# Moving the modulation's columns behind the memory's last products in a two-block transformer kernel

## The chip, the cores and the metric

One core of one Trainium2 chip runs the whole program. The metric is device time in microseconds (us) of one execution.

## What is computed

The program is two blocks in a row, for one sequence of 256 tokens of width 2048, in 32-bit floats. Everything below concerns the start of it. Cut to what matters there:

```
mem_n = rms_norm(mem, mem_norm_w)                       # 256 x 2048
k0, v0, k1, v1 = mem_n @ mem_k0, mem_n @ mem_v0, ...    # four 2048 x 512 matrices ("the memory's products")
mod = silu(c) @ w_ada + b_ada                           # 2048 x 6144, c is one vector
shift, scale, gate = split(mod, 3)
h = rms_norm(x, norm_gain) * (1 + scale) + shift
proj = h @ w_in                                         # 2048 x 8192 ("layer 1's products")
... attention, retention, w_out, x + gate * y, then the second block's two layers, which use k0..v1
```

The memory's products need nothing of the modulation, so they run first and cover the loading and adding up of w_ada. Layer 1's products need `h`, and with it shift and scale.

## The kernel before

**Products.** Every product on TensorE (PE) goes by chunks of a weight matrix of 512 KB: one DMA on SP's queue brings it into one of 7 slots of `raw` (`load_weights`, L393), ScalarE (ACT) rounds it into `w_hi` (`split_hi`, L414, instruction L418; 5 slots), VectorE (DVE) writes the rest into `w_lo` over the raw slot (`split_lo`, L420, instruction L422), and PE multiplies by both (L486 to L488 where the products have tokens as rows, L492 and L493 elsewhere). ACT and DVE split chunk n+3 while chunk n is multiplied (`AHEAD = 3`). SP asks for chunk n when PE is through chunk n-7.

**Units.** A chunk of PE's is here called a unit. The memory's products (`G_MEM`) are units 0 to 31, of 2 MB for each of the four matrices; layer 1's products begin with unit 32 (`G_SBQK0`), and their first 40 units use the first half of the rows of `h` only. In every unit, ACT, DVE and PE run a hook beside the chunk's work: `mem_hook_1` (L771) on ACT, `ada_hook` (L1299) on DVE, `mem_tail_hook` (L1890) on PE. Each engine runs its instructions in the order in which they were written.

**The modulation.** w_ada comes as 96 transfers of 512 KB ("modulation chunks") on POOL's queue (L615), into a ring of 6 tiles, each asked for when the sixth before it is used (semaphore `ada_used`). DVE adds each, weighted by silu(c), into `ada_sum` (L1257 for a first, L1260 for the others). The first 32 chunks are shift and scale of the first 8 tiles of `h` (half 0), the next 32 those of the other 8 tiles, the last 32 are the gate. `ada_units` (L1289) says how many are added by which unit. After a half's last chunk PE turns the sums into columns by 32 matmuls with one column (`modulation_columns`, L1881, instruction L1876), and `half_norm` on DVE and ACT makes 8 tiles of `h`: DVE reads the columns (L1278, L1279), computes a tile (L1157), ACT rounds it (L689), DVE writes the rest (L1166). A tile's L1166 comes two tiles later than its L1157, and the first product of layer 1 waits for tiles 0 to 3.

**The norm of x.** x comes as 4 transfers (L614) on POOL's queue, ahead of modulation chunks 10, 12, 14 and 16; ACT squares them in four groups (L659), POOL adds up three of them (L596, L598) between its transfers, PE sums over partitions (L1862), and ACT makes the inverse root (L677, L680).

In the memory's products the order of all this is a matter of unit numbers:

```
done.append(done[-1] + (3 <= u < units - 3) + (4 <= u < units - 4 and u % 4 == 0))   # ada_units, L1289
if u == MEM_UNITS - 4:                                                               # mem_tail_hook
    modulation_columns(0)
if u >= units - 3:                                                                   # ada_hook, and the like on ACT
    half_norm(half, u - (units - 3))
```

So before, one chunk is added in each of the units 3 to 28, and a second one in the units 4, 8, 12, 16, 20 and 24; PE's columns stand behind unit 28, and `half_norm(0)` is spread over the units 29 to 31.

Of the kernel before, what the change touches and what calls it, by code (L numbers as in the profile page):

```python
# [148 lines left out]
def build(nc, io):  # L149
    with ExitStack() as ctx:  # L150
# [411 lines left out]
        def _(sp):  # L562
# [14 lines left out]
            for g in ORDER:  # L577
                load_weights(sp, g, beside_first if g is G_MEM[0] else None)
                if g is G_SBQK:
                    sp.wait_ge(q["ada_cols"], 2)  # L580
                    sp.dma_start(con1[:, :], io["con1"]).then_inc(loaded["con1"], 16)
# [8 lines left out]
        def _(pool):  # L590
# [11 lines left out]
            for m, (half, k, part) in enumerate(ADA_ORDER):  # L602
# [5 lines left out]
                if m in (22, 25, 28):  # L608
                    add_squares(1, [(22, 25, 28).index(m)])
# [32 lines left out]
        def _(act):  # L642
# [128 lines left out]
            def mem_hook_1(unit):  # L771
                if unit in (0, 2, 4):
                    mem_hi(unit // 2 + 1)
                if unit in (0, 1, 3, 5):
                    norm_square(0, (0, 1, 3, 5).index(unit), mem_raw)
                if unit == 7:
                    mem_root()
                if unit in (17, 19, 21, 23):
                    act.wait_ge(loaded["x"], 64)
                    norm_square(1, (17, 19, 21, 23).index(unit), xT)  # L780
                if unit == 26:
                    norm_inverse_root(1)
                if unit >= MEM_UNITS - 3:
                    half_norm(0, unit - (MEM_UNITS - 3))
# [15 lines left out]
            for i, g in enumerate(G_MEM):  # L800
                run(g, at_units(8 * i, mem_hook_1), hook_first=False)
            for i, g in enumerate((G_SBQK0, G_RTQK0, G_SBV0)):
                run(g, at_units(16 * i, early_hook), hook_first=False)
# [343 lines left out]
        def _(dve):  # L1147
# [141 lines left out]
            def ada_units(units):  # L1289

                done = [0]
                for u in range(units):
                    if units == MEM_UNITS:
                        done.append(done[-1] + (3 <= u < units - 3) + (4 <= u < units - 4 and u % 4 == 0))
# [4 lines left out]
            def ada_hook(u0, units, half):  # L1299
                done = ada_units(units)  # L1300

                def hook(b, p):
                    if p % 2 == 0:
# [5 lines left out]
                        if u >= units - 3:  # L1309
                            half_norm(half, u - (units - 3))  # L1310
                return hook

            for i, g in enumerate(G_MEM):
                run(g, ada_hook(8 * i, MEM_UNITS, 0), hook_first=False)
            for i, g in enumerate((G_SBQK0, G_RTQK0, G_SBV0)):
# [529 lines left out]
        def _(pe):  # L1845
# [44 lines left out]
            def mem_tail_hook(i, p):  # L1890
# [13 lines left out]
                if u in (19, 21, 23, 25):  # L1904
                    sum_squares(1, [(19, 21, 23, 25).index(u)])
                if u == MEM_UNITS - 4:
# [386 lines left out]
```

## Time and profile before

| | us |
|---|---|
| time, median of 3 runs | 1797.61 (1795.02 to 1800.67) |
| time of the profiled execution | 1793.41 |
| its span, first to last instruction | 1791.2 |
| TensorE busy in the span | 1742.6 (97%) |
| VectorE busy | 1288.3 (72%) |
| ScalarE busy | 899.7 (50%) |
| GpSimd busy | 125.9 (7%) |
| mean granted TensorE clock | 0.991 of full |
| moved by DMA | 350.70 MB |

The busy shares are averages over the whole program. All of the change lies in its first 130 us, where they are different ones, so the rows below are nearly all of that stretch. Times in rows count from the start of the span; PE is TensorE, DVE VectorE, ACT ScalarE, POOL GpSimd, SP the engine that only issues transfers. A timeline's row may merge neighbours that overlap: "x2" is two instructions, and its second number is the time that they take together.

### The profile page before, as it was taken

How to read it: one execution, taken by the hardware profiler on the slowest of the kernel's cores; microseconds unless marked ns; L12 is line 12 of the kernel's file. 1: busy time of each engine (PE TensorE's matmuls, PEld its weight loads, DVE VectorE, ACT ScalarE, POOL GpSimd, SP SyncE). 2: the span in 40 equal slices, each digit the busy share in tenths (PEclk: the TensorE clock that was granted, in tenths of full speed). 3: DMA queues.
4: the chain of work that ended last, by engine and by line, in shares of the span. 5: the costliest groups of instructions: out<-in, count | busy, mean ns of one | idle time of the engine just before them, and what ended most of it. 6: DMA issues, size and time to landing. Idle time of an engine off the chain costs nothing.

```text
span 1791.2 us, 24344 instructions
## 1 busy us (share of the span) xinstructions
PE 1742.6 (97%) x9671; PEld 1496.0 (84%) x9671; DVE 1288.3 (72%) x1622; ACT 899.7 (50%) x1161; POOL 125.9 (7%) x151
## 2 busy tenths in 40 slices
PE   7989999999999999999999999899999999999997
PEld 6778888877888888888888888788888888888885
DVE  6889979785677756887676777965554766778644
ACT  6444443444466445665444556654444545566532
POOL 3321101000010100110000000000000000000000
PEclk9989999999999999999999999999999999999998
DMA  9979979774445566666544555555565564444552
GB/s 359 385 270 349 343 233 326 230 237 136 146 147 175 188 177 188 189 186 178 165 142 141 155 162 166 167 188 188 188 184 176 161 204 141 141 130 131 176 187 96
DMA packets 310400, 350.70 MB, mean 196 GB/s; under 512 B 11296, under 2 KB 284832, under 8 KB 310288
## 3 DMA queue, kind: packets, MB, share of 16 engines
q1 hardware_dynamic: 295728, 296.24, 53.8%
q0 software_dynamic: 14560, 52.89, 8.2%
q8 instruction: 78, 1.28, 0.3%
q14 instruction: 34, 0.28, 0.1%
HBM read 347.00 MB, written 2.10 MB: 195 GB/s over the span
## 4 chain that ended last, share of the span: by engine, by line
PE 67%; DVE 18%; ACT 6%; issue 5%; DMA 2%; SPq 0%; ACTq 0%; DVEq 0%
PE psG L492 37%; PE psG L493 19%; DVE w_lo L422 6%; ACT w_hi L418 3%; DMA raw<-in_mem_w 2%; PE psG L486 2%; PE psG L488 2%; PE psG L487 2%; DVE ada_sum L1260 1%; DVE P L1218 1%; DVE P L1213 1%; PE psH L1876 1%; DMA ada_ring<-in_w_ada 1%; PE psH L1862 1%; DVE gate_sum L1260 1%
## 5 line engine op out<-in xcount | busy, mean ns | idle before, releaser
L492 PE MATMUL psG<-xA,w_hi 128*128 128x512 f32 x2624 | 942.2, 402 | 4.2 <-DVE w_lo L422 3.7
L422 DVE TENSOR_TENSOR w_lo<-raw,w_hi 128x1024 fp32r<-128x1024 f32 (+1 forms) x560 | 688.5, 1240 | 245.5 <-ACT w_hi L418 244.0
L493 PE MATMUL psG<-xA,w_lo 128*128 128x256 f32 x2624 | 734.5, 280 | 0.0
L418 ACT ACTIVATE w_hi<-raw 128x1024 fp32r<-128x1024 f32 (+1 forms) x560 | 570.4, 1043 | 234.9 <-PE psG L493 167.3
L492 PEld LDWEIGHTS psG<-xA,w_hi 128*128 128x128 f32 x2624 | 492.4, 188 | 123.1 <-issue 10.5
L493 PEld LDWEIGHTS psG<-xA,w_lo 128*128 128x128 f32 x2624 | 495.5, 189 | 4.2 <-issue 3.4
L492 PE MATMUL psG<-yP,w_hi 128*128 128x512 f32 x960 | 337.2, 396 | 3.1 <-DVE P L1218 1.6
L493 PE MATMUL psG<-yP,w_lo 128*128 128x256 f32 x960 | 267.9, 279 | 0.0
L492 PEld LDWEIGHTS psG<-yP,w_hi 128*128 128x128 f32 x960 | 180.0, 187 | 45.9 <-DVE P L1218 1.9
L461 ACT ACTIVATE P<-psG 128x512 f32<-128x512 f32 (+2 forms) x103 | 60.9, 592 | 241.3 <-PE psG L493 241.0
L493 PEld LDWEIGHTS psG<-yP,w_lo 128*128 128x128 f32 x960 | 181.0, 189 | 0.2
L1213 DVE TENSOR_TENSOR P<-psG,P 128x512 f32<-128x512 f32 (+2 forms) x103 | 70.4, 684 | 114.7 <-ACT P L461 114.7
L1260 DVE SCALAR_TENSOR_TENSOR ada_sum<-ada_ring,silc,ada_sum 128x1024 f32<-128x1024 f32 x60 | 79.9, 1338 | 0.0
L596 POOL TENSOR_TENSOR W<-W 128x512 f32<-128x512 f32 x15 | 28.1, 1871 | 645.2 <-ACT W L659 645.2
L615 POOL DMA_DIRECT2D ada_ring<-in_w_ada x96 | 51.1, 533 | 305.8 <-DVE gate_sum L1260 124.0
L1233 DVE TENSOR_TENSOR xT<-psG,xT 128x512 f32<-128x512 f32 x32 | 22.1, 692 | 54.3 <-PE psG L493 53.8
L492 PE MATMUL psG<-xM,w_hi 128*128 128x512 f32 x128 | 49.4, 425 | 3.3 <-DVE w_lo L422 3.3
L486 PE MATMUL psG<-w_hi,xA 128*128 128x512 f32 x128 | 52.0, 406 | 0.0
L492 PE MATMUL psG<-xQ,w_hi 128*128 128x512 f32 x144 | 51.1, 399 | 0.0
L487 PE MATMUL psG<-w_lo,xA 128*128 128x512 f32 x128 | 50.6, 395 | 0.0
L488 PE MATMUL psG<-w_hi,xA 128*128 128x512 f32 x128 | 50.5, 395 | 0.0
L693 ACT ACTIVATE xA<-xT,vec 128x256 fp32r<-128x256 f32 x32 | 14.3, 501 | 52.0 <-DVE xT L1236 27.3
(325 smaller groups left out, 1789.9 us busy)
## 6 DMA issues: line engine op xcount, KB each, us to landing
raw<-in_w_in SPq DMA_DIRECT2D x360, 512.0 KB, 3.8
raw<-in_w_out SPq DMA_DIRECT2D x128, 512.0 KB, 3.4
ada_ring<-in_w_ada POOLq DMA_DIRECT2D x96, 512.0 KB, 6.3
raw<-in_mem_w SPq DMA_DIRECT2D x32, 512.0 KB, 10.1
raw<-in_w_uq SPq DMA_DIRECT2D x24, 384.0 KB, 3.3
raw<-in_w_ukv SPq DMA_DIRECT2D x32, 128.0 KB, 2.4
raw<-in_w_ukv SPq DMA_DIRECT2D x16, 256.0 KB, 3.3
P<-in_memT SPq DMA_DIRECT2D x4, 512.0 KB, 7.1
```

The costliest lines, as they stand in the source:

```text
L418: nc.scalar.activation(high(n), low(n, raw), ACT.Copy).then_inc(hi_ready, 1)
L422: nc.vector.tensor_tensor(low(n), low(n, raw), high(n), ALU.subtract).then_inc(lo_ready, 1)
L461: nc.scalar.activation(g.dst(b), product(g, b, 0), ACT.Copy).then_inc(copied, 1)
L486: nc.tensor.matmul(out, x_hi, hi[:, w], start=first, stop=False)
L487: nc.tensor.matmul(out, x_hi, lo[:, w], start=False, stop=False)
L488: last = nc.tensor.matmul(out, x_lo, hi[:, w], start=False, stop=end)
L492: nc.tensor.matmul(psG[:, bank + f, :], hi[:, w], x, start=first, stop=False)
L493: last = nc.tensor.matmul(psG[:, bank + f, S:2 * S], lo[:, w], x[:, 0:S], start=False, stop=end)
L596: nc.gpsimd.tensor_tensor(a[:, 0:512], a[:, 0:512], a[:, 512:1024], ALU.add).then_inc(q["nm_pair"], 1)
L615: pool.dma_start(ada_ring[slot][:, :], ada_rows(k, part, half)).then_inc(ada_loaded[slot], 16)
L1213: ins = v.tensor_tensor(out, product(g, b, 1), out, ALU.add)
L1260: v.scalar_tensor_tensor(out=out, in0=src, scalar=silc[:, k:k + 1], in1=out, op0=ALU.mult, op1=ALU.add).then_inc(ada_used, 1)
```

## The change

- `ada_units`: half 0's chunks are added one in each of the units 3 to 31, and a second one in the units 14, 19 and 24.
- PE's `modulation_columns(0)` stands behind unit 31 instead of unit 28.
- All three steps of `half_norm(0)`, on ACT and DVE, stand behind unit 31 instead of in the units 29, 30 and 31.
- The squares of x are taken by ACT in the units 17, 19, 22, 24 (before 17, 19, 21, 23), the third group added by POOL ahead of modulation chunk 27 (before 28), summed by PE in the units 21, 23, 25, 27 (before 19, 21, 23, 25), and the root taken in unit 28 (before 26).
- SP waits, ahead of its first transfer for layer 1 (chunk 32), until 24 modulation chunks have been used.

No instruction is added or taken away but SP's wait.

```diff
             load_memory(0)
             for g in ORDER:
+                if g is G_SBQK0:
+                    sp.wait_ge(ada_used, 24)
                 load_weights(sp, g, beside_first if g is G_MEM[0] else None)
...
-                if m in (22, 25, 28):
-                    add_squares(1, [(22, 25, 28).index(m)])
+                if m in (22, 25, 27):
+                    add_squares(1, [(22, 25, 27).index(m)])
...
-                if unit in (17, 19, 21, 23):
+                if unit in (17, 19, 22, 24):
                     act.wait_ge(loaded["x"], 64)
-                    norm_square(1, (17, 19, 21, 23).index(unit), xT)
-                if unit == 26:
+                    norm_square(1, (17, 19, 22, 24).index(unit), xT)
+                if unit == 28:
                     norm_inverse_root(1)
-                if unit >= MEM_UNITS - 3:
-                    half_norm(0, unit - (MEM_UNITS - 3))
...
             for i, g in enumerate(G_MEM):
                 run(g, at_units(8 * i, mem_hook_1), hook_first=False)
+            for step in range(3):
+                half_norm(0, step)
...
                     if units == MEM_UNITS:
-                        done.append(done[-1] + (3 <= u < units - 3) + (4 <= u < units - 4 and u % 4 == 0))
+                        done.append(done[-1] + (3 <= u) + (u in (14, 19, 24)))
...
-                        if u >= units - 3:
+                        if half and u >= units - 3:
                             half_norm(half, u - (units - 3))
...
             for i, g in enumerate(G_MEM):
                 run(g, ada_hook(8 * i, MEM_UNITS, 0), hook_first=False)
+            for step in range(3):
+                half_norm(0, step)
...
-                if u in (19, 21, 23, 25):
-                    sum_squares(1, [(19, 21, 23, 25).index(u)])
-                if u == MEM_UNITS - 4:
+                if u in (21, 23, 25, 27):
+                    sum_squares(1, [(21, 23, 25, 27).index(u)])
+                if u == MEM_UNITS - 1:
                     modulation_columns(0)
```

DVE's order around half 0's last chunks. Before (`ada_ring_67` is the ring's tile of chunk 31, the last of half 0; L422 are splits, L1278 and L1279 read the columns):

```order
L422 TENSOR_TENSOR w_lo<-raw,w_hi 128x1024 [waits hi_ready]
L1260 SCALAR_TENSOR_TENSOR ada_sum<-ada_ring_67,silc,ada_sum 128x1024 [waits ada_used,ada_loaded1]
L422 TENSOR_TENSOR w_lo<-raw,w_hi 128x1024 [waits hi_ready]
L1278 TENSOR_TENSOR mod<-psH,vec 128x2x8 [waits ada_cols]
L1279 SCALAR_TENSOR_TENSOR gs<-mod,vec 128x8 [waits dve_step]
L1157 SCALAR_TENSOR_TENSOR W<-xT,gs,W 128x256 [waits nm_rs,dve_step]
L1157 SCALAR_TENSOR_TENSOR W<-xT,gs,W 128x256 x2
```

And in the changed kernel, whose lines from L577 on have moved by two or more:

```order
L1262 SCALAR_TENSOR_TENSOR ada_sum<-ada_ring_71,silc,ada_sum 128x1024 [waits ada_used,ada_loaded5]
L422 TENSOR_TENSOR w_lo<-raw,w_hi 128x1024 [waits hi_ready]
L1262 SCALAR_TENSOR_TENSOR ada_sum<-ada_ring_66,silc,ada_sum 128x1024 [waits ada_used,ada_loaded0]
L422 TENSOR_TENSOR w_lo<-raw,w_hi 128x1024 [waits hi_ready]
L1262 SCALAR_TENSOR_TENSOR ada_sum<-ada_ring_67,silc,ada_sum 128x1024 [waits ada_used,ada_loaded1]
L1215 TENSOR_TENSOR memkv<-psG,memkv 128x512 [waits copied]
L1220 TENSOR_TENSOR memkv<-memkv,P 128x512 [waits nm_rs,dve_step]
L1280 TENSOR_TENSOR mod<-psH,vec 128x2x8 [waits ada_cols]
L1281 SCALAR_TENSOR_TENSOR gs<-mod,vec 128x8 [waits dve_step]
```

Before, the last addition stands behind the split of chunk 31. Now it stands behind the split of chunk 34, a chunk of layer 1's weights, and the landing of the memory's last block (L1215, L1220) stands between it and the columns.

PE's order around the columns, before (`xM` is the normed memory, so the products behind are unit 29's):

```order
L492 MATMUL psG<-xM,w_hi 128x512
L493 MATMUL psG<-xM,w_lo 128x256
L1876 MATMUL psH<-con,ada_sum 128x1 [waits ada_used]
L1876 MATMUL psH<-con,ada_sum 128x1 x15
L492 MATMUL psG<-xM,w_hi 128x512 [waits lo_ready,nm_lo]
```

And in the changed kernel (`xA` is `h`, so the products behind are unit 32's):

```order
L492 MATMUL psG<-xM,w_hi 128x512
L493 MATMUL psG<-xM,w_lo 128x256
L1880 MATMUL psH<-con,ada_sum 128x1 [waits ada_used]
L1880 MATMUL psH<-con,ada_sum 128x1 x15
L492 MATMUL psG<-xA,w_hi 128x512 [waits lo_ready,nm_lo,vector_landed]
```

The products behind the columns are now the ones that wait, by `nm_lo`, for the tiles of `h` that are made from the columns.

## Rows read from the trace of the kernel before

**Rows 1.** Windows: stretch and length, then busy us of PE, PEld, DVE, ACT, POOL; clock; DMA share; GB/s.

```profile
60.00:110.00 50.00, 44.29 (x203) 36.92 (x204) 48.59 (x39) 24.84 (x28) 21.02 (x26) 0.93 1.04 380
118.00:126.00 8.00, 8.00 (x36) 7.21 (x37) 5.32 (x13) 3.22 (x7) 0.00 (x0) 0.66 0.03 10
130.00:240.00 110.00, 110.00 (x617) 95.68 (x616) 97.02 (x98) 50.90 (x61) 15.32 (x29) 0.98 0.93 322
```

**Rows 2.** Waits, 40 to 125 us: who waited for whom, total us, times, longest.

```profile
ACT w_hi L418 <- DMA raw<-in_mem_w: 27.6, 11, 5.0
PE psG L492 <- DVE w_lo L422: 3.3, 1, 3.3
PE psH L1862 <- POOL W L598: 2.8, 1, 2.8
PE psH L1876 <- DVE ada_sum L1260: 2.5, 1, 2.5
```

**Rows 3.** PE's timeline: start, length, instruction, [idle before it and releaser].

```profile
59.16 0.28 PE L493 MATMUL psG<-xM,w_lo 128*128 128x256 f32 x1
62.75 0.76 PE L492 MATMUL psG<-xM,w_hi 128*128 128x512 f32 x1 [3.32 <-DVE w_lo L422]
...
102.09 0.58 PE L492 MATMUL psG<-xM,w_hi 128*128 128x512 f32 x1
...
110.48 0.28 PE L493 MATMUL psG<-xM,w_lo 128*128 128x256 f32 x1
113.25 6.98 PE L1876 MATMUL psH<-con,ada_sum 128*128 128x1 f32 x32 [2.49 <-DVE ada_sum L1260]
120.10 0.77 PE L492 MATMUL psG<-xM,w_hi 128*128 128x512 f32 x1
...
130.05 0.40 PE L492 MATMUL psG<-xA,w_hi 128*128 128x512 f32 x1
```

**Rows 4.** Windows again, columns as in rows 1: two stretches at a lower clock.

```profile
62.00:69.00 7.00, 6.25 (x19) 5.32 (x20) 7.00 (x7) 3.40 (x5) 1.58 (x3) 0.51 1.04 382
113.20:123.40 10.20, 10.15 (x42) 9.67 (x43) 3.94 (x9) 2.19 (x5) 0.53 (x1) 0.50 0.46 169
```

**Rows 5.** Chain of waits, 36 to 62 us: start, length, what.

```profile
42.50 17.76 DMA raw<-in_mem_w
60.29 1.06 ACT w_hi L418
```

**Rows 6.** DMA queues, 36 to 61 us (q0 is POOL's, q1 SP's): packets, MB, share.

```profile
DMA packets 4391, 9.53 MB, mean 381 GB/s; under 512 B 297, under 2 KB 2293, under 8 KB 4390
q0 software_dynamic: 1755, 6.35, 67.2%
q1 hardware_dynamic: 2635, 3.16, 36.9%
```

**Rows 7.** DMA total and issues, 0 to 106 us.

```profile
DMA packets 21017, 39.44 MB, mean 372 GB/s; under 512 B 1203, under 2 KB 12083, under 8 KB 21012
```

**Rows 8.** DVE's timeline: one unit's pace, and the start of half_norm.

```profile
96.61 1.22 DVE L422 TENSOR_TENSOR w_lo<-raw,w_hi 128x1024 fp32r<-128x1024 f32 x1
97.74 1.28 DVE L1260 SCALAR_TENSOR_TENSOR ada_sum<-ada_ring,silc,ada_sum 128x1024 f32<-128x1024 f32 x1
98.94 1.22 DVE L422 TENSOR_TENSOR w_lo<-raw,w_hi 128x1024 fp32r<-128x1024 f32 x1
...
109.46 0.69 DVE L1213 TENSOR_TENSOR memkv<-psG,memkv 128x512 f32<-128x512 f32 x1
...
122.67 0.48 DVE L1166 SCALAR_TENSOR_TENSOR xA<-W,mod,xA 128x256 fp32r<-128x256 f32 x1
```

**Rows 9.** PE's timeline where half 1's columns run, and the products behind them.

```profile
232.41 3.63 PE L1876 MATMUL psH<-con,ada_sum 128*128 128x1 f32 x32
235.90 0.61 PE L486 MATMUL psG<-w_hi,xA 128*128 128x512 f32 x1
```

**Rows 10.** PE by line, 9 to 131 us: the sums of squares.

```profile
L1862 PE MATMUL psH<-W,con 128*128 128x256 f32 x28 | 7.4, 382 | 2.8 <-POOL W L598 2.8
```

## The prediction

> **What bounds the kernel now.** The change lies before 130 us, so the page's busy shares (PE 97%) say little; I read the windows first, for who is full in that stretch. From 60 to 110 us two things are: the DMA engines (share 1.04, 380 GB/s) and DVE (48.59 of 50 us), while PE is busy 44.29 of 50 at a mean clock of 0.93 [rows 1]. From 130 us on PE is busy 110.00 of 110, with DVE at 97.02. So a microsecond saved before the first product of layer 1 (130.05 [rows 3]) stays saved, and one lost stays lost.
>
> Next the waits, for what PE lacks. It stops three times: 3.3 us for the split of a chunk, 2.8 us for POOL's sums of squares, 2.5 us for the last modulation chunk; ACT's waits for memory chunks come to 27.6 us in 11 waits [rows 2]. The timeline gives them places. The first is between units 14 and 15 (59.44 to 62.75). Units 26 to 28 show the undisturbed pace: 24 pairs of L492 and L493 from 102.09 to 110.76, 0.35 us a pair, about 2.80 us a unit at the full clock. Then the third stop, the columns (6.98 us from 113.25) and the first pairs of unit 29 [rows 3]. The clock was low (0.51 and 0.50 of full, the 1.2 GHz level) from 62.0 to 69.0, behind the first stop, and from 113.2 to 123.4, behind the third and through the columns [rows 4]. At the full level the same 32 matmuls took 3.63 us, spacing 3.49 [rows 9].
>
> Last the chain, for what made unit 15 late: chunk 15's transfer, 17.76 us from issue to landing at 60.29, then ACT [rows 5]. In that stretch POOL's queue moved 6.35 MB and SP's 3.16 [rows 6]: memory chunks starve behind modulation chunks and x.
>
> **What the change costs and gives.**
>
> *One addition per unit, early part.* By the end of unit 11 two chunks fewer have been used (9 instead of 11), so two fewer have been asked for, and x's last quarter, tied to chunk 16, isn't yet either: three transfers of 0.524 MB, 1.57 MB, at 0.381 MB a us (381 GB/s [rows 6]) 4.1 us. Chunk 15 lands at about 56.2 instead of 60.29, its split is done by 58.5, and PE doesn't stop at 59.44. That gives back the 3.3 us, and the low clock behind it: from 62.75 to about 69.0 PE ran at half its rate [rows 3, 4], 6.2 us for 3.1 us of work. Bounds for the sum: nothing (the stop stays) and 6.4. I take all of it.
>
> *The squares.* Same instructions, one or two units later; the sums that PE waited 2.8 us for come a unit later against ACT's square. The 2.8 us go if ACT and POOL are in time, otherwise they stay; I take them as gone. POOL's third addition holds back chunk 27 by the 3 to 4 us that it takes, which its use in unit 27 doesn't feel.
>
> *End of the memory's products, by PE alone.* From 59.4: 17 units of 2.80, 47.6, and the second set of sums. There are 28 matmuls L1862 in 7.4 us busy [rows 10], overlapping; the half of them that is this norm's costs about 2.6 on PE. So unit 31 ends at 109.6 at the earliest. Before it would have been 110.76 + 3 x 2.80 = 119.2 without columns, so up to 9.6 us lie here.
>
> *By DMA.* Chunk 31 must land. With it: 32 memory chunks, 9 transfers of memory, x and constants, and about 31.7 modulation chunks; 72.7 x 0.524 and the 0.17 of the vectors are 38.3 MB. Before, 39.44 MB had moved by 106 us [rows 7], so 38.3 at about 103.0. Then ACT 1.06, the split 1.14 and unit 31: 108.0. PE's own 109.6 is later.
>
> *The last addition.* DVE's order now has four units behind chunk 31's rounding: split and addition, 2.33 us a unit (96.61 to 98.94 [rows 8]), 9.3 us. From 104.1 that ends at 113.4; if two more modulation chunks go ahead of chunk 31 it lands at 105.7 and the end is 116. DVE alone, never short of data, from chunk 15's rounding at 57.3: 20 units 46.6, three second additions 3.6, two landings of 1.4 (0.69 each instruction [rows 8]), so 110.3. I take 114.3, nearest to the DMA's row since the DMA is full until then.
>
> *Columns.* PE has then been idle since 109.6, 4.7 us. The stop of 3.32 and the one of 2.49 were both followed by the low clock [rows 3, 4], so I price the columns at 6.98 and not 3.49: they end at 121.3. Bounds 3.5 and 7.0. The memory's last landing on DVE lies beside them.
>
> *half_norm, now bare.* It hid behind units 29 to 31. From the columns' end to DVE's second L1166 at 122.67 it took 2.4 us; two more tiles follow at once, in the order L1157, L1166, L1157, L1166, where the starts are some 0.4 us apart: 1.6, and 0.48 for the last to end. With the semaphore 4.6 us: the first product of layer 1 starts at 125.9. The other four tiles take 2.4 more, inside PE's first two units.
>
> *Restart at the low clock.* Unit 29 began at 120.10 and had the low clock until 123.4, which cost 1.6; behind the first stop it cost 3.1 [rows 3, 4]; and behind half 1's columns, without any idle time, the first product was slow too (0.61 us [rows 9], against 0.40 at 130.05 [rows 3]). I take 1.6, bounds 1.6 and 3.1.
>
> Sum: 114.3 + 7.0 + 4.6 + 1.6 = 127.5, against 130.05: **2.5 us less**. What is gained in the memory's products, 9.6 us, is paid back for the most part by PE's wait, the columns and the bare half_norm.
>
> *SP's wait.* Chunk 32 could be asked for once PE is through unit 25, at about 92. The 24th use is the first addition of unit 24, behind the split of chunk 27, which lands about then: it holds SP for some 0 to 4 us. Nothing for memory is behind it on SP's queue, only layer 1's chunks. Their splits are in DVE's last three units, so the cost is in the range of the last addition above.
>
> *Afterwards.* The DMA engines idle from 118 to 126 (share 0.03 [rows 1]) with all slots full; the same 43.7 MB will be in by about then, so layer 1 starts with full slots as before, and PE runs as before.
>
> The profiled execution would take 1793.41 - 2.5 = 1790.9. It lies 4.2 under the median of the three runs, so for the median I say 1797.61 - 2.5 = 1795.1. A measurement of this kernel can tell about 0.3%, 5.4 us, from no change.
>
> One rule bears on who gets the DMA engines. Here POOL's queue moved twice the bytes of SP's, in packets of 3.6 KB against 1.2 KB (6.35 MB in 1755, 3.16 in 2635 [rows 6]). The Trainium skill, "DMA: Bandwidth & Descriptors", section on queues, rings and completion order, says that each engine goes round the queues that have work, one packet at a time. By that rule, the queue with small rows loses whenever the other has anything, and a chunk of SP's lands behind all that POOL has asked for; the trace agrees in direction. That is the rival below that speaks against the change.
>
> **Rivals.**
>
> *Chunk 34 is late (slower).* The last addition stands behind chunk 34's split. If all 38 modulation chunks that can be asked for by then go ahead of it, 35 + 38 + 9 transfers are 43.2 MB, at 115.8 by the rate above; ACT, split, addition end it at 119.2. Then 7.0 + 4.6 + 3.1 give 133.9, 3.9 us worse: 1801.5. For it: the 17.76 us of chunk 15, and SP's added wait, which makes chunk 34 later. Against: POOL is given a chunk only per use, and while DVE waits for chunk 34 it uses none. It decides from the point where chunk 34 lands after about 113.
>
> *The DMA keeps up (faster).* The last addition comes at DVE's own 110.3 with PE idle for under 1 us; the columns run at the full clock (3.5), half_norm 4.6, restart 3.1: 121.5, 8.5 us less: 1789.1. For it: half 1's columns ran at full clock behind products. Against: DMA share 1.04 and ACT's 27.6 us of waits.
>
> *The early part doesn't change.* Chunk 15 stays late, as the modulation chunks saved there are few. Unit 31 ends near 119, columns 3.5 to 7.0, then 4.6 and 3.1: 130.2 to 133.7, about 2 us worse: 1799.6.
>
> **How the numbers follow.** Chances: forecast 0.50, DMA keeps up 0.24, chunk 34 late 0.20, early part unchanged 0.06. Faster by over 0.3% takes nearly all of the second and a little of the first, 0.25. Slower by over 0.3% needs chunk 34's case with a new stop beside it, 0.13. The rest, 0.62, is no difference. The range is from 1788.5, just under the faster case, to 1802.5, just above the chunk 34 case; what is left is a stop that I haven't seen.
>
> **What would show it.** In the changed profile: no idle time of PE before unit 15, and clock at full from 62 to 69; the last PE product on `xM` at 109 to 111 instead of 130.0; then an idle time of 3 to 6 us ended by `ada_sum`, 32 column matmuls of 7 us at clock 0.5, and an idle time of 4 to 5 us ended by DVE's `xA`; the first product on `xA` at about 126. If the columns take 3.5 us, or the idle time before them is under 1 us, the faster rival holds; if DVE waits for ACT in the last three units and ACT for `in_w_in`, the slower one. A first product on `xA` before 121 or after 134 would make the prediction wrong.

## The result, and the profile after

| | before | changed |
|---|---|---|
| first measurement, median us | 1798.24 (1792.65 to 1803.14, 8 runs) | 1804.51 (1800.07 to 1807.05, 8 runs) |
| profiled execution, us (span) | 1793.41 (1791.2) | 1804.36 (1802.2) |
| mean granted clock | 0.991 | 0.987 |

The ratio is 1.0031 (95% interval 1.0016 to 1.0046): 0.31% slower, where 0.14% faster was forecast and 1802.5 us was the upper end of the range. Two more measurements of the changed kernel, below, gave 0.9990 (0.9974 to 1.0007) and 1.0003 (0.9989 to 1.0016). So 5.6 us are not the size of the change; the question is what is.

The windows of the changed kernel, columns as in [rows 1]:

```profile
60.00:110.00 50.00, 48.09 (x237) 39.38 (x237) 46.82 (x38) 23.79 (x26) 19.82 (x26) 1.00 1.04 378
62.00:69.00 7.00, 7.00 (x33) 5.78 (x33) 6.66 (x7) 2.61 (x3) 1.58 (x3) 1.00 1.04 387
116.00:123.70 7.70, 6.97 (x32) 6.90 (x32) 1.97 (x3) 0.00 (x0) 0.53 (x1) 0.53 0.83 304
123.70:128.40 4.70, 0.10 (x2) 0.12 (x1) 4.58 (x13) 2.83 (x6) 0.00 (x0) 0.50 0.00 0
128.40:133.60 5.20, 5.20 (x17) 4.42 (x18) 4.87 (x9) 2.91 (x4) 0.49 (x1) 0.50 0.00 0
```

From 60 to 110 us PE is busy 48.09 us instead of 44.29 at the full clock instead of 0.93, and the low clock from 62 to 69 us is gone [rows 1, 4]. The three rows behind are the price: columns at the low clock, no products for 4.6 us, products at the low clock for 5.2 us more. PE's timeline shows the same places (columns as in [rows 3]):

```profile
112.17 0.28 PE L493 MATMUL psG<-xM,w_lo 128*128 128x256 f32 x1
116.73 6.99 PE L1880 MATMUL psH<-con,ada_sum 128*128 128x1 f32 x32 [4.28 <-DVE ada_sum L1262]
128.31 0.77 PE L492 MATMUL psG<-xA,w_hi 128*128 128x512 f32 x1 [4.60 <-issue]
234.88 3.62 PE L1880 MATMUL psH<-con,ada_sum 128*128 128x1 f32 x32
316.73 2.52 PE L1880 MATMUL psH<-con,gate_sum 128*128 128x1 f32 x16 [1.25 <-DVE gate_sum L1262]
439.56 2.46 PE L1880 MATMUL psH<-con,gate_sum 128*128 128x1 f32 x16 [0.78 <-DVE P L1368]
```

Unit 31 ends at 112.45; before, unit 28 ended at 110.76 [rows 3], so three more units are done in 1.7 us, where they take 8.4: 6.7 us are gained. Then it is given back: 4.28 us for the last addition, 6.99 us of columns, 4.60 us for `h`. The first product of layer 1 starts at 128.31 instead of 130.05, but the clock stays low until about 133.6 and costs 2.6 us more (half of 5.3). At equal clock that is 130.9: **0.9 us later than in this profile of before**. A second profile of before, c2 below, starts 1.1 us earlier.

The last three rows serve as marks further on: the columns of half 1, and the gate's first and second ones. The same three groups of columns stood, before, at

```profile
232.41 3.63 PE L1876 MATMUL psH<-con,ada_sum 128*128 128x1 f32 x32
...
314.13 1.95 PE L1876 MATMUL psH<-con,gate_sum 128*128 128x1 f32 x16 [1.18 <-DVE gate_sum L1260]
433.77 1.95 PE L1876 MATMUL psH<-con,gate_sum 128*128 128x1 f32 x16 [0.78 <-DVE P L1364]
```

So the changed kernel is 2.5 us late at the first mark, 2.6 at the second, 5.8 at the third, and 11.0 at the end of the span. Of the 11.0 us only 0.9 arose where the change is. The jump from 2.6 to 5.8 has a row of its own, and so has one behind the third mark; windows of the changed kernel, and of the kernel before at the same work:

```profile
318.00:325.00 7.00, 7.00 (x26) 6.15 (x26) 3.19 (x4) 1.06 (x1) 0.53 (x1) 0.52 0.78 265
440.80:447.60 6.80, 6.80 (x20) 4.74 (x19) 2.53 (x3) 0.00 (x0) 1.27 (x2) 0.50 0.00 0
```

```profile
314.00:321.00 7.00, 6.87 (x42) 5.95 (x43) 4.41 (x6) 1.29 (x2) 1.06 (x2) 1.00 0.87 299
437.50:444.30 6.80, 6.80 (x36) 5.39 (x35) 4.77 (x6) 3.25 (x4) 0.00 (x0) 1.00 0.26 79
```

PE went to the 1.2 GHz level behind the gate's columns (matmuls of one column, ahead of them a wait), where before it kept 2.4 GHz: some 3.3 us each. Whether these belong to the change or to the execution was the first thing to find out.

### The profile page after: what moved, and what is told of

Same layout as the page of the kernel before. It is cut to its first block, busy times and chain, and to the rows that moved or that the text cites. A ratio compares the mean times of both kernels' runs of the same rounds, so it can differ in the third digit from the quotient of the medians.

```text
span 1802.2 us, 24345 instructions
## 1 busy us (share of the span) xinstructions
PE 1751.7 (97%) x9671; PEld 1500.3 (83%) x9671; DVE 1289.2 (72%) x1622; ACT 900.1 (50%) x1161; POOL 123.8 (7%) x151
## 3 DMA queue, kind: packets, MB, share of 16 engines
q8 instruction: 78, 1.28, 0.3%
## 4 chain that ended last, share of the span: by engine, by line
PE 67%; DVE 18%; ACT 7%; issue 5%; DMA 3%; SPq 0%; ACTq 0%; DVEq 0%
PE psG L492 37%; PE psG L493 19%; DVE w_lo L422 6%; ACT w_hi L418 3%; PE psG L486 2%; PE psG L488 2%; PE psG L487 2%; DMA raw<-in_mem_w 2%; DMA raw<-in_w_in 1%; DVE P L1220 1%; DVE P L1215 1%; PE psH L1880 1%; DVE gate_sum L1262 1%; PE psH L1866 1%; DVE P L1509 1%
## 5 line engine op out<-in xcount | busy, mean ns | idle before, releaser
L492 PE MATMUL psG<-xA,w_hi 128*128 128x512 f32 x2624 | 950.8, 405 | 8.8 <-issue 5.2
L422 DVE TENSOR_TENSOR w_lo<-raw,w_hi 128x1024 fp32r<-128x1024 f32 (+1 forms) x560 | 689.7, 1242 | 250.1 <-ACT w_hi L418 248.6
L493 PE MATMUL psG<-xA,w_lo 128*128 128x256 f32 x2624 | 738.1, 281 | 0.0
L492 PEld LDWEIGHTS psG<-xA,w_hi 128*128 128x128 f32 x2624 | 495.8, 189 | 130.7 <-issue 15.4
L493 PEld LDWEIGHTS psG<-xA,w_lo 128*128 128x128 f32 x2624 | 498.7, 190 | 4.3 <-issue 3.5
L492 PE MATMUL psG<-yP,w_hi 128*128 128x512 f32 x960 | 339.0, 398 | 3.1 <-DVE P L1220 1.6
L493 PE MATMUL psG<-yP,w_lo 128*128 128x256 f32 x960 | 268.6, 280 | 0.0
L492 PEld LDWEIGHTS psG<-yP,w_hi 128*128 128x128 f32 x960 | 180.1, 188 | 47.2 <-DVE P L1220 1.9
L493 PEld LDWEIGHTS psG<-yP,w_lo 128*128 128x128 f32 x960 | 181.1, 189 | 0.2
L1215 DVE TENSOR_TENSOR P<-psG,P 128x512 f32<-128x512 f32 (+2 forms) x103 | 70.4, 683 | 117.0 <-ACT P L461 117.0
L492 PE MATMUL psG<-xQ,w_hi 128*128 128x512 f32 x144 | 50.2, 392 | 0.0
L492 PE MATMUL psG<-xM,w_hi 128*128 128x512 f32 x128 | 45.5, 400 | 0.5 <-DVE w_lo L422 0.5
```

The costliest lines, as they stand in the source:

```text
L422: nc.vector.tensor_tensor(low(n), low(n, raw), high(n), ALU.subtract).then_inc(lo_ready, 1)
L492: nc.tensor.matmul(psG[:, bank + f, :], hi[:, w], x, start=first, stop=False)
L493: last = nc.tensor.matmul(psG[:, bank + f, S:2 * S], lo[:, w], x[:, 0:S], start=False, stop=end)
L1215: ins = v.tensor_tensor(out, product(g, b, 1), out, ALU.add)
```

## The experiments

"Start of layer 1" in the table is the first product on `xA`, plus half of the time for which the clock stayed low behind it. "Clock by marks" is the granted clock of three stretches, 225 to 245, 305 to 330 and 430 to 452 us, which hold the three groups of columns. The measurements rest on 12 runs each, but for the first (8), b3 (8) and b4 (6).

| kernel | ratio to before (95% interval) | last addition done, us | start of layer 1, us | clock by marks |
|---|---|---|---|---|
| before, first profile | 1 | 113.2 | 130.05 | 0.91, 1.00, 1.00 |
| before again (c2) | 0.9995 (0.9979 to 1.0012) | 112.1 | 128.97 | 1.00, 1.00, 0.92 |
| changed, first | 1.0031 (1.0016 to 1.0046) | 116.7 | 128.31 + 2.6 = 130.9 | 0.91, 0.86, 0.84 |
| changed again (a1) | 0.9990 (0.9974 to 1.0007) | 116.5 | 127.85 + 3.1 = 130.9 | 1.00, 1.00, 1.00 |
| changed, third (b1) | 1.0003 (0.9989 to 1.0016) | 116.8 | 128.22 + 3.0 = 131.2 | 0.91, 1.00, 1.00 |
| before, shifted (a2) | 1.0013 (0.9996 to 1.0030) | 114.5 | 132.10 | 0.91, 1.00, 1.00 |
| no SP wait (a3) | 1.0001 (0.9985 to 1.0017) | 116.5 | 128.11 + 2.4 = 130.5 | 0.83, 0.86, 0.84 |
| spread only (a4) | 0.9981 (0.9965 to 0.9997) | 111.8 | 128.63 | 0.91, 1.00, 1.00 |
| columns only (b2) | 0.9984 (0.9970 to 0.9999) | 113.8 | 128.58 + 1.5 = 130.1 | 0.91, 0.93, 0.92 |
| four additions in unit 28 (b3) | 0.9968 (0.9951 to 0.9985) | 112.7 | 121.85 + 3.0 = 124.9 | 0.91, 0.93, 0.92 |
| changed, PE filled (b4) | 0.9955 (0.9939 to 0.9972) | 116.5 | 125.10 | 0.91, 0.93, 1.00 |
| before, PE filled (c3) | 0.9980 (0.9964 to 0.9996) | 113.3 | 128.49 | 1.00, 1.00, 1.00 |
| b3 and filled (c1) | 0.9960 (0.9943 to 0.9977) | 112.4 | 121.61 | 0.91, 0.93, 1.00 |

### Are the late low-clock stretches the change's?

**a1 and b1: the changed kernel again, no edit.**

> The changed kernel once more, for a second profile of it. In its first profile the span is 11.0 us longer than before: about 1.0 us at the start of layer 1's products, 1.5 us by a slower pace of the products up to 240 us, and 6.6 us by two stretches of low TensorE clock (317.92 and 440.80 us, each 6.83 us long) that begin right behind the gate's column matmuls and that the profile of before doesn't have. Theory 'place in time': where the columns lie against the clock's changes is fixed by the program, so both stretches are there again, within 0.2 us of the same times, and the median is 4 to 8 us over before's. Theory 'chance': they are drawn anew in each execution; this profile then has other ones, and the median of five lies anywhere from 0 to 7 us over before's.

> The changed kernel a third time. Its first measurement was 0.31% over before's (interval 0.16% to 0.46%), its second 0.10% under (0.26% under to 0.07% over), with profiles that differ in where the TensorE clock fell: at 116.54, 239.42, 317.92 and 440.80 in the first, at 116.93 and 1137.52 in the second. Theory 'small and constant, the rest drawn': layer 1 starts 0.8 to 1.0 us later than before at the same product in this profile too, the falls behind 240 us are other ones again, and the median lies between 2 us under and 6 us over before's. Rival 'place in time, fixed by the program': the falls are those of the first profile.

Medians 1796.74 us against 1798.61 (1.9 us under before's, where 0 to 7 over was expected), and 1801.39 against 1800.48. Start of layer 1 and last addition repeat within 0.3 us, but neither profile has the stretches at 318 and 441 us, and both have one at about 1137, which the first doesn't; a1 has, at the same work,

```profile
317.00:324.00 7.00, 7.00 (x36) 5.34 (x35) 2.88 (x3) 1.66 (x3) 0.53 (x1) 1.00 0.85 293
440.00:447.00 7.00, 7.00 (x42) 6.07 (x41) 4.49 (x5) 2.77 (x4) 0.00 (x0) 1.00 0.51 149
```

"Fixed by the program" falls: the same program keeps the full clock behind the same columns in one execution and not in another. The gate's columns start at 314.67 and 434.31 in a1, at 314.94 and 434.60 in b1: 0.5 to 0.8 us behind the first profile of before, where the first profile of the changed kernel was 2.6 and 5.8 behind.

**a2: the kernel before, shifted.** Ahead of the products of layer 1:

```diff
+            for _ in range(6):
+                mm(psH[:, BC, 0:S], ones, C("ones", S), start=True, stop=True)
             for i, g in enumerate((G_SBQK0, G_RTQK0, G_SBV0)):
```

> The kernel before with six matmuls more (128x256 of constants into an unused bank) ahead of the first product of layer 1, 2.6 us by the 0.43 us that such a matmul takes in the sums of squares. Nothing else is changed. Theory 'place in time': everything behind is 2.6 us later, as in the changed kernel, so the two stretches of low clock at about 318 and 441 us appear and the time is 2.6 + 6.6, some 9 us over before's (7 to 11). Rival 'the change itself' (later modulation additions leave VectorE or the DMA queues otherwise filled in layer 1): no new stretch, 2.6 us over before's (1.5 to 4).

Median 1801.32 against 1798.61: ratio 1.0013 (0.9996 to 1.0030), 2.7 us in the medians, which is the price of the six matmuls. Its first two marks lay later than the changed kernel's in its first profile (236.35, 317.73), and the two stretches did not come: in this one profile, the shift alone did not bring them. Its span was 8.9 us above before's all the same, of which 3.6 had arisen by the third mark (437.39): what varies lies further behind as well.

**c2: the kernel before again, no edit.**

> The kernel before once more, for a second profile. Theory 'drawn anew in each execution': layer 1 starts within 0.6 us of its first profile, but behind 240 us low-clock stretches come that its first profile didn't have (at about 314, 437 or 1135 us), and its span differs by 2 to 10 us; the median stays within 0.2% of before's. Rival: the stretches are those of the first profile (236 us only), and only the changed kernels have others.

1796.35 against 1797.59. One of the stretches is in this profile of the kernel before, behind the gate's second columns:

```profile
314.00:321.00 7.00, 7.00 (x41) 5.66 (x40) 3.61 (x5) 1.06 (x1) 0.63 (x2) 1.00 0.90 305
437.00:444.00 7.00, 7.00 (x28) 4.62 (x27) 4.63 (x5) 2.19 (x3) 0.00 (x0) 0.81 0.19 50
```

The forecast of a second one held (0.78 from 1132 to 1139 us), its span came only 0.3 us above the first profile's, under the 2 to 10 expected, and its layer 1 starts 1.1 us earlier than in the first, where 0.6 was the limit. The stop before unit 15, on which the prediction's largest gain rested, isn't in this profile. Its clock was low early, 0.79 from 24 to 32 us against 1.00 in the first; a4 and c1 have the same. In the ten profiles at full clock there, the stop stands in all four with before's additions (before, a2, b2, c3: 2.8 to 3.3 us) and in none of the six with those of the changed kernel in the units up to 27 (changed, a1, b1, a3, b3, b4).

### What each part does to the start of layer 1

**a3: the changed kernel without SP's wait.**

```diff
-                if g is G_SBQK0:
-                    sp.wait_ge(ada_used, 24)
```

> The changed kernel without SP's wait for 24 used modulation chunks. In the changed kernel's profile the last three units' splits wait for chunks 32 to 34 of layer 1's weights (ScalarE waits 3.2, 4.1 and 1.5 us for them) and the last addition ends at 116.67 instead of the 114.3 forecast. Theory 'SP's wait delays chunks 32 to 34': without it the last addition ends 1 to 2.5 us earlier and the first product of layer 1 with it (126 to 127.3 instead of 128.31). Rival 'the DMA engines are full anyway': no change of the last addition beyond 0.5 us. For the total, every 1 us of shift may move the two stretches of low clock in or out, so the total can change by 3 to 7 us either way.

SP asks for chunk 32 at 93.82 instead of 97.15, and the last addition starts at 115.20 instead of 115.39. The rival's number holds: the wait costs nearly nothing. But not for its reason alone: DVE was busy 36.37 of 36.40 us from 80 to 116.4 in this run, so weights that come sooner find no free DVE (see b3). The total, 1799.70 against 1798.61, is that of before.

**a4: only the additions spread.** On the kernel before:

```diff
-done.append(done[-1] + (3 <= u < units - 3) + (4 <= u < units - 4 and u % 4 == 0))
+done.append(done[-1] + (3 <= u < units - 3) + (u in (14, 17, 20, 22, 24, 26)))
```

> One part of the change alone, on the kernel before: second additions in units 14, 17, 20, 22, 24 and 26 instead of 4, 8, 12, 16, 20 and 24, with the columns still behind unit 28 and half_norm beside units 29 to 31. Theory 'the spread gives, the move takes': TensorE's stop of 3.3 us before unit 15 and the low clock behind it go (6.4 us), VectorE ends the last addition at 106 to 108 instead of 113.2, and the first product of layer 1 starts at 123 to 126 instead of 130.05, 4 to 7 us less. Rival 'the stop only moves': the DMA engines are full, so the chunks saved early are missing later, and the first product starts within 1.5 us of 130.05. The total follows, 4 to 7 us under before's or the same, if no stretch of low clock comes or goes behind 240 us; each that comes costs 3.3.

Start 128.63: 1.4 us ahead of the first profile of before, 0.3 of the second. The forecast of 123 to 126 fails, the rival is nearer. The first stop is gone, but this profile has the early low clock with which c2 lacks it too, so a4 alone doesn't show that the spreading removed it. And PE's timeline has

```profile
78.27 1.22 PE L1862 MATMUL psH<-W,con 128*128 128x256 f32 x2 [3.61 <-POOL W L598]
...
111.88 6.98 PE L1876 MATMUL psH<-con,ada_sum 128*128 128x1 f32 x32 [2.40 <-DVE ada_sum L1260]
```

a stop for POOL's sums, which is longer now, with a low clock behind it (0.57 from 77 to 85 us), and the last addition is only 1.4 us earlier.

**b2: only the columns and half_norm moved.** The changed kernel with additions, squares and SP of before:

```diff
-                        done.append(done[-1] + (3 <= u) + (u in (14, 19, 24)))
+                        done.append(done[-1] + (3 <= u < units - 3) + (4 <= u < units - 4 and u % 4 == 0))
...
-                if u in (21, 23, 25, 27):
-                    sum_squares(1, [(21, 23, 25, 27).index(u)])
+                if u in (19, 21, 23, 25):
+                    sum_squares(1, [(19, 21, 23, 25).index(u)])
```

> The other part of the change alone: columns and all of half_norm behind unit 31, but modulation additions, squares and SP as in the kernel before (last addition in unit 28, at about 113). TensorE still stops 3.3 us before unit 15 and 2.8 us for the sums of squares, so unit 31 ends at 118 to 119.5; no wait for the additions. Theory 'the move takes what the spread gives': then columns (3.5 us at the full clock, up to 7), 4.6 us of half_norm without products and 1.6 to 3.1 us for the low clock behind it put the start of layer 1 0 to 4 us behind before's at the same product. If the move cost nothing (rival), it would be 3 us or more ahead, since the 2.5 us wait for the last addition is gone.

```profile
120.36 3.63 PE L1878 MATMUL psH<-con,ada_sum 128*128 128x1 f32 x32
128.58 0.76 PE L492 MATMUL psG<-xA,w_hi 128*128 128x512 f32 x1 [4.59 <-issue]
```

With no wait ahead of them the columns take 3.63 us. Unit 31 ended at about 120.4, a little above the 118 to 119.5 expected. The bare half_norm (4.59 us) and 1.5 us of low clock eat what the missing wait gave: start 130.1, equal to that of before's first profile, 1.1 us behind its second. The move by itself is worth nothing at this place.

**b3: the last additions ahead of layer 1's splits.** On the changed kernel:

```diff
-                        done.append(done[-1] + (3 <= u) + (u in (14, 19, 24)))
+                        done.append(done[-1] + (3 <= u < 28) + (u in (14, 19, 24)) + 4 * (u == 28))
```

> The changed kernel with modulation chunks 28 to 31 added together in unit 28, ahead of the splits of chunks 32 to 34, instead of one behind each of these splits. Theory 'the last additions are held by the splits of layer 1's chunks and by ScalarE's waits for their transfers': the last addition ends at 112 to 113.5 instead of 116.67, TensorE waits less than 1 us for it instead of 4.28, the columns run at the full clock at least in part, and the first product of layer 1 starts at 121 to 125 instead of 128.3; against before, layer 1 is 3 to 7 us ahead. Rival 'the modulation chunks themselves arrive no earlier' (VectorE would wait for DMA in the additions): the last addition ends after 115.

DVE's timeline, then PE's:

```profile
107.79 4.87 DVE L1262 SCALAR_TENSOR_TENSOR ada_sum<-ada_ring,silc,ada_sum 128x1024 f32<-128x1024 f32 x4
112.57 3.49 DVE L422 TENSOR_TENSOR w_lo<-raw,w_hi 128x1024 fp32r<-128x1024 f32 x3
```

```profile
112.71 3.73 PE L1880 MATMUL psH<-con,ada_sum 128*128 128x1 f32 x32 [0.16 <-DVE ada_sum L1262]
121.85 0.77 PE L492 MATMUL psG<-xA,w_hi 128*128 128x512 f32 x1 [5.41 <-issue]
```

Additions 28 to 31 run back to back, so their data was there; in the changed kernel it was the splits ahead of them that held them. ACT waited for the weights of these splits, as its timeline in the changed kernel says of chunks 32 to 34:

```profile
105.39 1.06 ACT L418 ACTIVATE w_hi<-raw 128x1024 fp32r<-128x1024 f32 x1 [3.16 <-DMA raw<-in_w_in]
110.58 1.06 ACT L418 ACTIVATE w_hi<-raw 128x1024 fp32r<-128x1024 f32 x1 [4.13 <-DMA raw<-in_w_in]
113.16 1.06 ACT L418 ACTIVATE w_hi<-raw 128x1024 fp32r<-128x1024 f32 x1 [1.52 <-DMA raw<-in_w_in]
```

But DVE hardly felt it. Its splits of chunks 31 to 34 in the changed kernel, the last addition, and a window of a1:

```profile
106.56 1.22 DVE L422 TENSOR_TENSOR w_lo<-raw,w_hi 128x1024 fp32r<-128x1024 f32 x1
...
108.89 1.22 DVE L422 TENSOR_TENSOR w_lo<-raw,w_hi 128x1024 fp32r<-128x1024 f32 x1
...
111.67 1.23 DVE L422 TENSOR_TENSOR w_lo<-raw,w_hi 128x1024 fp32r<-128x1024 f32 x1 [0.37 <-ACT w_hi L418]
...
114.25 1.23 DVE L422 TENSOR_TENSOR w_lo<-raw,w_hi 128x1024 fp32r<-128x1024 f32 x1 [0.16 <-ACT w_hi L418]
115.39 1.28 DVE L1262 SCALAR_TENSOR_TENSOR ada_sum<-ada_ring,silc,ada_sum 128x1024 f32<-128x1024 f32 x1
```

```profile
80.00:116.50 36.50, 32.24 (x170) 26.77 (x168) 36.47 (x31) 16.72 (x20) 13.67 (x19) 1.00 1.04 368
```

DVE stood idle 0.53 us for ACT in these units, and in a1 and b1 not at all: from 80 to 116.5 us it was busy 36.47 of 36.50 in both, and the last addition came no earlier. So DVE's own work sets that point, and what b3 takes from ahead of it is three splits, 3.5 us, and the 0.5 of waiting: 116.7 less 4.0 is the 112.7 measured.

Four additions moved, and the start goes from 130.9 to 124.9, the time to 0.32% under before's.

### What the low clock costs at the move

**b4: the changed kernel with PE kept at work.**

```diff
                 if u == MEM_UNITS - 1:
+                    for _ in range(18):
+                        mm(psH[:, BC, :], xM[:, 0, 0:NP], xM[:, 1, :], start=True, stop=True)
                     modulation_columns(0)
+                    for _ in range(12):
+                        mm(psH[:, BC, :], xM[:, 0, 0:NP], xM[:, 1, :], start=True, stop=True)
```

> The changed kernel with idle time of TensorE filled: 18 products of 128x512 on the memory's tiles into an unused bank ahead of the columns (3.9 us at the full clock, in the wait of 4.28 us) and 12 behind them (2.6 us, in the 4.6 us wait for half_norm). Theory 'the low clock is half of the price of the move': the clock stays full through most of the columns, which take 3.5 to 4.5 us instead of 6.99, the first product of layer 1 starts at 124.5 to 126 instead of 128.3 and without slow products behind it, and layer 1 is 3 to 6 us ahead of the changed kernel's. Rival 'the columns bring the clock down by themselves', as at 236 us before where no idle time preceded them: then the 12 products behind them run at the low clock (5.2 us), they end after half_norm, and the start is 127.5 or later.

```profile
112.78 4.25 PE L1912 MATMUL psH<-xM 128*128 128x512 f32 x18
116.88 3.63 PE L1880 MATMUL psH<-con,ada_sum 128*128 128x1 f32 x32
120.36 4.60 PE L1915 MATMUL psH<-xM 128*128 128x512 f32 x12
...
125.10 0.47 PE L492 MATMUL psG<-xA,w_hi 128*128 128x512 f32 x1
```

The last addition is where it was, but the columns take 3.63 us instead of 6.99, and the products behind run at the full clock: the start is 125.1 instead of 130.9. So of the 14.2 us from the columns' start to 130.9, 5.8 were clock. The rival was half right too: behind the columns the clock fell all the same (0.79 from 117 to 125 us), the 12 products took 4.60 us instead of 2.6, and just fitted into the wait.

**c3: the same on the kernel before,** 10 such products ahead of the columns behind unit 28.

```diff
                 if u == MEM_UNITS - 4:
+                    for _ in range(10):
+                        mm(psH[:, BC, :], xM[:, 0, 0:NP], xM[:, 1, :], start=True, stop=True)
                     modulation_columns(0)
```

> The kernel before with 10 products on the memory's tiles into an unused bank ahead of the columns behind unit 28, 2.2 us in the wait of 2.49 us for the last addition. Theory 'low clock is a price that the kernel before pays too': the columns take 3.5 to 5 us instead of 6.98, unit 29 starts at 116.7 to 118.5 instead of 120.10, and layer 1 starts 2 to 5 us earlier; the median is 2 to 5 us under before's. Rival 'VectorE and the DMA engines set the start of layer 1': the time won is waited away in units 29 to 31, and layer 1 starts within 1 us of before's.

The columns take 4.10 us, unit 29 starts at 117.30 instead of 120.10, but at the low clock, which stays until 123.4 (0.50 from 117.0 to 123.4). Start 128.49, 1.6 us ahead of the first profile of before, 0.5 of the second: less than the 2 to 5 expected. The median is 2.9 us under before's, inside the 2 to 5 expected; the start shows only 0.5 to 1.6 of it.

**c1: b3 and 14 such products behind the columns.**

```diff
                 if u == MEM_UNITS - 1:
                     modulation_columns(0)
+                    for _ in range(14):
+                        mm(psH[:, BC, :], xM[:, 0, 0:NP], xM[:, 1, :], start=True, stop=True)
```

> The version with modulation chunks 28 to 31 added in unit 28, and 14 products on the memory's tiles into an unused bank behind the columns, in the wait for half_norm (5.4 us there). Theory 'the two gains add up': the first product of layer 1 starts at about 121.9 as without the 14 products, but at the full clock, which was worth 2.6 us, so layer 1 is 7 to 8 us ahead of before's at the same product (5.4 without), and the median is 6 to 9 us under before's. Rival 'what the clock gives at the start it takes behind 240 us': layer 1 starts as said, but the median stays at that of the version without the 14 products, some 6 us under before's.

```profile
112.47 3.94 PE L1880 MATMUL psH<-con,ada_sum 128*128 128x1 f32 x32 [0.25 <-DVE ada_sum L1262]
116.27 4.82 PE L1913 MATMUL psH<-xM 128*128 128x512 f32 x14
...
121.61 0.47 PE L492 MATMUL psG<-xA,w_hi 128*128 128x512 f32 x1 [0.53 <-issue]
```

Start 121.61 at the full clock, 8.4 us ahead of the first profile of before and 7.4 of the second. Median 1790.12 us against 1797.59, 0.40% less (0.23% to 0.57%). The start is 3.3 us ahead of b3's, which is what b3's low clock behind the columns cost (3.0). The 6.0 us of b3 and the 5.8 of b4 don't add up in full, since b3's columns already ran at the full clock. By the time b4, b3 and c1 can't be told apart (0.45%, 0.32%, 0.40%, overlapping). All three are under before's by more than their intervals, and their ratios lie below all three of the changed kernel's.

## Why the prediction was wrong

**Right.** Most of the mechanism, and its places. The stop before unit 15 and the low clock behind it went, in all six profiles that can be compared (see c2). PE waits for `ada_sum` behind unit 31 (4.28 us, 3 to 6 forecast), the columns run at the low clock (6.99, forecast 7.0), then PE waits for `h` (4.60, forecast 4.6). SP's wait was priced at 0 to 4 us inside the last addition's range; removing it moved that addition by 0.2 us.

**Mis-sized: "The last addition ... I take 114.3".** It was done at 116.7 (116.5 and 116.8 in the two other profiles), 2.4 us later, above even the 116 that I gave as its late end. The sum let DVE's last four units begin as soon as chunk 31 was rounded, at 104.1. ACT had rounded it by 101.4, so the data was early; but DVE took up its split only at 106.56, since it was full: 26.00 of 26 us from 79 to 105. The term that was too small is the one for DVE alone, 110.3. DVE split chunk 16 at 57.57; 19 units, three second additions and two landings, at the prices of the prediction, end at 108.2. To that come 3.7 us in which DVE did wait for ACT, 3.1 of them before 76 us, and some 4.3 us because splits and additions took longer beside POOL's sums of squares (last section): 116.2, near the 116.7 measured. b3 shows the same from the other side: without the three splits ahead, the additions are done at 112.7, with PE no longer waiting.

The rival "chunk 34 is late" had this point at 119.2. Its sign came, ACT waiting 3.16, 4.13 and 1.52 us for chunks 32 to 34, but it cost DVE 0.53 us here and nothing in a1 and b1.

**Mis-sized: "Restart at the low clock. I take 1.6".** It was 2.6, inside the bounds of 1.6 to 3.1; in the two other profiles 3.1 and 3.0.

The two sum to 3.4 us and turn the 2.5 us gain into the 0.9 us loss at the start of layer 1. The other missed numbers had no weight: unit 31 ended at 112.45 and not 109.6 (PE had small stops at 77, 83 and 87 us, 1.7 us in all, and a unit takes 2.83 us at 0.353 a pair, not 2.80, which makes 0.5 over 17 units; the other 0.6 I didn't trace), but PE waited for the addition anyway.

**Failed: "Afterwards ... PE runs as before", and with it the range.** The prediction took one execution's time behind 130 us as fixed. In the profiles of these kernels that part changes by itself: stretches of low clock of about 1.7 to 3.4 us' cost come and go at 236, 437 and 1135 us, in both kernels, and products have two paces (below). Behind its start the changed kernel's first profile lost 10.1 us more than the first of before; a1's lost about 1.5 (span 1793.6).

The three ratios, weighed by their 8, 12 and 12 runs, average 1.0005, or 0.9 us. The start of layer 1 shows 0.9 us against before's first profile and about 2 against its second. That agreement is worth no more than the intervals of 0.15%: a loss at the start is shown, a loss of the whole isn't.

Two things stay open. All eight runs of the first measurement lie above 1800 us, while 9 of a1's 12 lie below it, but only 3 of b1's 12. The granted clock tells part of it: its mean is 0.9884 over the eight runs, 0.9905 over a1's and 0.9893 over b1's. By an estimate, 0.001 of 1800 us is 1.8 us, so this is 3.8 of the 7.0 us between the mean times of the first eight runs and of a1's; for the rest there is no cause on record. And the stretch behind the gate's first columns (305 to 325 us) stands in six of the eight profiles whose columns of half 0 run behind unit 31 (changed, a3, b2, b3, b4, c1, not a1 and b1), but in none of the five that have them behind unit 28 (before, c2, a2, a4, c3). Whether the move makes it more likely was not tested.

**The shape of the gain.** Singly, the parts give 1.4 us (a4) and nothing (b2); together they lose 0.9, all against before's first profile. With the second as the base it is 0.3 gained, 1.1 lost and 1.9 lost. So 1.1 to 2.2 us more are lost together than singly. The likely reason is that the last additions are drawn out to unit 31, behind layer 1's splits: neither part has that, and the whole has; b3, which takes only this back, gains 6.0 us.

The Trainium skill's rule of packet-wise turns between queues ("DMA: Bandwidth & Descriptors", section on queues, rings and completion order) was the ground for the rival "chunk 34 is late". From 97 to 112.5 us SP asked for seven chunks of layer 1's weights; they took 8.2 to 13.5 us to land while POOL's queue was fed. The rival put all that POOL had asked for ahead of chunk 34. Turns alone don't say that: from 36 to 61 us SP's queue moved more packets than POOL's, 2635 against 1755, only smaller ones [rows 6]. No run here gave SP's queue larger rows, so the rule itself was not tried.

## What to carry to other kernels

When work is spread up to a deadline, look at what stands ahead of its last piece on the same engine: here one list of numbers decided whether the last additions stood behind three splits of another stage, and that was worth 6 us. Where an engine is full, its own list of instructions gives the time, from the point where it last had to wait, and not the landing of its last input: here the input was 5 us early. When a serial step (a small reduction, a norm) is taken out from beside products, price the clock as well as the wait: 5.8 of 14.2 us here were TensorE at 1.2 GHz, and unneeded products in the gaps gave them back. And where the effect sought is 0.3%, compare the place in two profiles of each kernel before trusting one ratio: the start of layer 1 repeated to 0.3 us in the changed kernel and to 1.1 in the one before, while the total of one program varied by 10.

## What the runs showed of the hardware

**The same program keeps the full clock at a place in one execution and loses it in the next.** Columns of one-column matmuls, with or without a wait ahead, were followed by the low clock in some profiles and not in others: behind half 1's columns in ten of the thirteen profiles of all kernels, at the first gate columns in six, at the second in five. In b4 it fell behind columns that ran at full clock with products right before and behind.

**Two paces at the same granted clock.** Pairs of L492 and L493 start 0.347 us apart in the first profile of before, and 0.353 in that of the changed kernel, both at clock 1.00:

```profile
138.03 0.39 PE L492 MATMUL psG<-xA,w_hi 128*128 128x512 f32 x1
...
138.72 0.39 PE L492 MATMUL psG<-xA,w_hi 128*128 128x512 f32 x1
```

```profile
138.53 0.40 PE L492 MATMUL psG<-xA,w_hi 128*128 128x512 f32 x1
...
139.24 0.40 PE L492 MATMUL psG<-xA,w_hi 128*128 128x512 f32 x1
```

0.69 against 0.71 us for two pairs. From 150 to 210 us every one of the thirteen profiles keeps to one of the two: seven to the faster (before, b1, a3, a4, b3, c1, c3), six to the slower (c2, changed, a1, a2, b2, b4), so each kernel has both. Over layer 1's first 100 us this makes the 1.6 us by which the changed kernel fell back from 0.9 us at its start to 2.5 at the first mark. b1, the same program, didn't fall back (first mark at 233.40, 1.0 us behind before's), and c2, the kernel before, did: from 1.1 us ahead at its start to 0.7 behind (233.08). What sets the pace isn't known; no run was made for it.

**DVE's instructions took longer while POOL added.** POOL adds up squares of x from 83.14 to 86.26 us in the changed kernel's first profile. DVE's addition and split beside it:

```profile
83.35 2.31 DVE L1262 SCALAR_TENSOR_TENSOR ada_sum<-ada_ring,silc,ada_sum 128x1024 f32<-128x1024 f32 x1
85.59 1.75 DVE L422 TENSOR_TENSOR w_lo<-raw,w_hi 128x1024 fp32r<-128x1024 f32 x1
```

Elsewhere in this stretch they take 1.28 and 1.22 us. The same stands beside POOL's two other sums (a split of 1.90 and an addition of 1.75 us from 75.20, an addition of 2.32 and a split of 1.75 from 89.59), 4.3 us more in all. The kernel before has it too (2.32 and 1.76 us at 81.76).
